# Moving the operand parts fh and fl, and every buffer declared behind them, by 32 bytes in SBUF

## What is computed

```python
x = first_block(x, c, ...)   # adaLN, gated conv + pooling mixer, conv GELU feed-forward
h = x
for i in range(2):
    mix = gated_deltanet(h, ...) if i == 0 else moba_attention(h, ...)
    h = layer_norm_2(ALPHA * h + mix, ...)
    h = layer_norm_2(ALPHA * h + swiglu(h, f_w13[i], f_w2[i]), ...)

def swiglu(x, w13, w2):
    g, u = jnp.split(x @ w13, 2, axis=-1)
    return (jax.nn.silu(g) * u) @ w2
```

## Time and profile before

| | us |
|---|---|
| median of 3 runs | 1084.91 |
| lowest and highest | 1083.35, 1088.65 |
| the profiled execution's own time | 1086.5 |
| its span, first to last instruction | 1084.7 |
| PE busy in the span | 1051.5 (97%), 7748 matmuls |
| DVE busy | 776.6 (72%) |
| ACT busy | 599.3 (55%) |
| DMA moved | 195.47 MB, mean 180 GB/s |
| mean granted TensorE clock | 0.994 of full speed |

### The profile page before, as it was taken

How to read it: one execution, slowest core, us unless ns; L and a number is a source line. 1 busy time by engine, 2 the same in 40 slices (tenths; PEclk the granted TensorE clock), 3 DMA queues, 4 the chain that set the end, 5 groups by cost and what they waited for, 6 DMA issues and landing times.

```text
span 1084.7 us, 18886 instructions
## 1 busy us (share of the span) xinstructions
PE 1051.5 (97%) x7748; PEld 988.8 (91%) x7748; DVE 776.6 (72%) x1327; ACT 599.3 (55%) x1029; POOL 1.3 (0%) x13
## 2 busy tenths in 40 slices
PE   7999998999999999989999999999999999999999
PEld 7999997999999988889987899999899878999997
DVE  7989998788878778676768655555689766555555
ACT  5577555665556567652455654544565656545543
POOL 0000000000000000000000000000000000000000
PEclk9999999999999989999999999999999999999999
DMA  9996574566766523351223555656465436565511
GB/s 373 418 361 201 178 245 156 175 216 238 239 219 198 193 80 115 107 166 60 84 92 110 200 177 192 194 176 195 141 211 173 124 116 247 176 192 190 181 60 39
DMA packets 58021, 195.47 MB, mean 180 GB/s; under 512 B 10320, under 2 KB 10704, under 8 KB 57680
## 3 DMA queue, kind: packets, MB, share of 16 engines
q1 hardware_dynamic: 56784, 194.21, 53.1%
q10 hardware_dynamic: 1152, 0.07, 0.1%
HBM read 192.94 MB, written 1.31 MB: 179 GB/s over the span
## 4 chain that ended last, share of the span: by engine, by line
PE 73%; DVE 18%; ACT 7%; issue 2%; DMA 1%; ACTq 0%; POOL 0%; DVEq 0%; POOLq 0%; SPq 0%
PE ps L551 63%; DVE lo L1748 6%; PE ps L848 3%; ACT hi L1166 2%; PE ps L634 2%; DVE raw L1735 2%; DVE ev L1980 1%; DVE ev L1977 1%; DVE B L2158 1%; DVE sm L1925 1%; PE ps L727 1%; DVE ev L1987 0%; ACT ev L1345 0%; DVE xa L1759 0%; DVE B L1816 0%
## 5 line engine op out<-in xcount | busy, mean ns | idle before, releaser
L1748 DVE TENSOR_TENSOR lo<-raw,hi 128x1024 fp32r<-128x1024 f32 x311 | 376.6, 1221 | 141.9 <-ACT hi L1166 141.2
L551 PE MATMUL ps<-hh,hi 128*128 128x256 f32 x1568 | 445.4, 284 | 9.6 <-DVE hl L1793 3.1
L551 PE MATMUL ps<-hl,hi 128*128 128x256 f32 x1568 | 440.1, 281 | 0.0
L551 PE MATMUL ps<-hh,lo 128*128 128x256 f32 x1568 | 439.9, 281 | 0.0
L1166 ACT ACTIVATE hi<-raw 128x1024 fp32r<-128x1024 f32 x311 | 323.4, 1052 | 50.2 <-PE ps L551 44.6
L551 PEld LDWEIGHTS ps<-hh,hi 128*128 128x128 f32 x1568 | 297.2, 190 | 15.0 <-issue 6.1
L551 PEld LDWEIGHTS ps<-hl,hi 128*128 128x128 f32 x1568 | 297.2, 190 | 1.6
L551 PEld LDWEIGHTS ps<-hh,lo 128*128 128x128 f32 x1568 | 297.0, 189 | 0.0
L551 PE MATMUL ps<-hi,hh 128*128 128x512 f32 x184 | 75.0, 408 | 2.9 <-DVE hl L2022 2.5
L551 PE MATMUL ps<-hi,fh 128*128 128x512 f32 x192 | 76.3, 397 | 0.0
L551 PE MATMUL ps<-lo,fh 128*128 128x512 f32 x192 | 75.9, 395 | 0.0
(11 more groups left out here) (283 smaller groups left out, 1272.2 us busy)
## 6 DMA issues: line engine op xcount, KB each, us to landing
raw<-in_w SPq DMA_DIRECT2D x359, 512.0 KB, 4.3
B<-in_t SPq DMA_DIRECT2D x2, 512.0 KB, 4.8
xa<-in_x SPq DMA_DIRECT2D x1, 1024.0 KB, 11.2
B<-in_r SPq DMA_DIRECT2D x1, 1024.0 KB, 6.1
out<-h SPq DMA_DIRECT2D x4, 256.0 KB, 2.0
cst<-in_c SPq DMA_DIRECT2D x1, 864.0 KB, 9.3
vec<-in_v SPq DMA_DIRECT2D x1, 328.5 KB, 7.7
ev<-between SPq DMA_DIRECT2D x1, 128.0 KB, 2.6
```

What stands on the lines that cost most here:

```text
L551: m = g.matmul(o, l, r, start=first and n == 0, stop=last and n == 2, skip_group_check=True)
L1748: g.tensor_tensor(lo[:, j % SPLIT, :], raw[:, PLACE[j] % RAW, :], hi[:, j % SPLIT, :].bitcast(F), ALU.subtract).then_inc(*up("lo", j))
```

## The change

`gap1` grows from 8 to 16 words, so `fh`, `fl` and everything declared behind them lie 32 bytes further. The four passes of `idle_rows` are taken out. No other instruction, wait or DMA is added, removed or moved.

```diff
         hh = sb("hh", [P, NC, S], FR)
         hl = sb("hl", [P, NC, S], FR)
-        gap1 = sb("gap1", [P, 8])
+        gap1 = sb("gap1", [P, 16])
         fh = sb("fh", [P, 4, S], FR)
         fl = sb("fl", [P, 4, S], FR)
...
             ffn_tokens("w131", "w21", "w13r1", "x5", [[at("att_lo", 4 + 2 * c + half) for half in range(2)] for c in range(2)])
 
-            def idle_rows(shift):
-                wh, wl = (w[:, 0, shift:shift + 512] for w in (hi, lo))
-                for k in range(2):
-                    three(bank[4][:, :], wh, wl, hh[:, k, 0:P], hl[:, k, 0:P], True, True, flip=True)
-
-            for shift in (0, 8, 16, 24):
-                idle_rows(shift)
-
```

## The result

The changed kernel took **1088.59 us** (median of 22 runs, 1085.74 to 1091.47), the kernel before 1086.05 us (22 runs, 1081.33 to 1090.43). The ratio is **1.0023, with a 95% interval of 1.0013 to 1.0033**: some 2.5 us slower, 1.4 to 3.6. That is no tie, but it lies within the 0.5% that I called no change. The forecast was 1085.1 us against 1084.9, +0.2 us. Of the 3.5 us between 1085.1 and 1088.59 the kernel before accounts for 1.1: its median was 1084.91 over three runs and is 1086.05 over 22. The change accounts for the rest.

The account below looks back on a forecast made before the run. PE's matmul streams were taken to bound the kernel from 296 us in the first layer and throughout the later two. Terms -0.3 + 0.5 = +0.2 us on a median of 1084.91 gave 1085.1 us, range 1081 to 1090.

Parts of the forecast that it names:

- the forecast's own case: Down units run as with `hh`: +0.2 us, 1085.1 us for the median; chance 0.60.
- rival (c): Down units of all three layers at 120 and 240 ns, tiles behind at 117.9: +7.5 us, 1092.4; chance 0.13.
- the prediction's own signs: Wrong if down units took 2.72 or 2.88 us for 24, or long-row tiles 2.83; right at 2.80.
- Where a longer matmul costs time: First layer from 296 us, second and third throughout: one for one; before 296 us DVE covers it.
- fh and fl moving, first layer: 264 matmuls of down units behind 296 us go from 117.9 to 116.7 ns: -0.3 us, bounds -1.2 and +0.6.
- all of these now run at 117.9: The first layer's 11 down units behind 296 us, before the change, taken at 117.9 ns a matmul.
- The tiles behind them: Tiles after the down units keep their pattern: 0; if all fell into the slower one, +2.6 us.
- fh and fl stationary: Later layers and half the delta rule's output, 576 matmuls: +0.5 us, bounds -2.6 (228 ns) and +4.3 (240 ns).
- Everything behind fl: Buffers 32 bytes further, for DVE, ACT, DMAs and matmuls with both operands there: 0.
- idle_rows, 0: 24 matmuls at the end that nobody waits for, hidden by DVE's normalisation: 0, or 0.03 us if wrong.
- Rival (a): Addresses don't matter, or a rounding of the layout swallows the 32 bytes: 1084.9 us; chance 0.15.
- Rival (b): Moving reads at 113.3 ns, stationary ones as the last pass of `idle_rows`: -3.8 us, 1081.1; chance 0.12.

Follow-up runs that it names:

- e3: Kernel before without `idle_rows`, `fh` and `fl` 32 bytes further (place 96), buffers behind them 128 bytes further; ratio 1.0022.
- e8: Kernel before without `idle_rows`, `fh` and `fl` moved to place 32, that of `hh`, the rest in place modulo 128; ratio 0.9991.
- e1: Kernel before with only `gap1` grown to 16 words, `idle_rows` kept; ratio 1.0012.
- e12: The kernel of e2 run once more for its profile; no ratio, one run of 1086.76 us.
- e6: Kernel before without `idle_rows`, `gap0` at 40 and `gap1` at 24 words: `hh` and `hl` at place 96, `fh` and `fl` at 192; ratio 1.0086.
- e7: Kernel before without `idle_rows`, `gap0` and `gap1` at 16 words: `hh` and `hl` at place 0, `fh` and `fl` still at 64; ratio 1.0090.
- e4: Kernel before without `idle_rows`, `fh` and `fl` in place, only the buffers behind them 32 bytes further; ratio 0.9999.
- e2: Kernel before with only `idle_rows` taken out; ratio 0.9998.
- e9: Kernel before without `idle_rows`, two views of longer `fh` and `fl` buffers: first layer 192/64 modulo 256, other uses 128/0; ratio 1.0020.
- e11: Kernel before without `idle_rows`, two views of longer `fh` and `fl` buffers: first layer 224/96 modulo 256, other uses 192/64; ratio 0.9998.
- e5: Kernel before without `idle_rows`, `gap0` at 32 words and no `gap1`: `hh` and `hl` at place 64, as `fh` and `fl`; ratio 1.0024.

## Why the prediction was right, and which steps failed

**The time fell into the range, and it was no change of over 0.5%; the forecast's own case did not come.** I had the units behave as `hh` does, +0.2 us. They behaved as in rival (c) for the moving operand, and the change cost 2.5 us. The bounds caught it, the chosen values didn't. By the prediction's own signs it was wrong: down units of 2.86 us, near the 2.88 that it named, and tiles of 2.83 and more in a long row. That the time held is owed to the width of the range and to how few matmuls without slack the change touches, and in that it was luck.

- *Where a longer matmul costs time*: right. From the first down unit to 296 us the layer took 90.49 us after 90.58; behind it the loss came through whole. By the chains, DVE's normalisation begins 78.77 to 79.81 us after the start of the piece in the four executions with `fh` at 64, and 80.72 to 80.77 in the three with it at 96.
- *fh and fl moving, first layer, -0.3 us*: failed, twice. The row of `hh` was chosen because it has the same place modulo 64, so that 96 would act as 32. e3 and e8 refute it: 119.7 ns at 96, 117.0 at 32. The upper bound, the 120 ns of `idle` in the earlier trace rows, was the right row. And "all of these now run at 117.9" held for one execution of the kernel. Over four executions at that place the 11 units have a mean of (113.5 + 117.9) / 2 = 115.7 ns. With it the term is 264 x (119.7 - 115.7) = +1.06 us.
- *The tiles behind them, left at 0*: too low. Behind 296 us 16 tiles of the first layer's ran at 117.8 after the change (18 in e1, 16 in e3), and none in the kernel before (two in e12). 16 x 24 x 1.1 ns = +0.42 us. With the term above that is 1.48 us, against 1.46 measured. The two later layers' tiles did not follow: none of them reached 117.5.
- *fh and fl stationary, +0.5 us*: right, a little high. 576 x 0.59 ns = +0.34 us by the distances, +0.29 by the stretches. The 240 ns of rival (c) did not come; 229.2 in e6 and 226.7 in e7 show that distances about the low bound of 228 exist, for other places.
- *Everything behind fl, 0*, and *idle_rows, 0*: right, as far as e4 and e2 can tell, each to some 1.5 us.
- *Rival (a), addresses don't matter*: falls with e6 and e7. *Rival (b), the new place suits PE*: falls; distances near its 113.3 and 228 ns, 114.2 and 229.2, appear at 192, not at 96.

The mechanism that I gave, two reads of one engine that get in each other's way, is still only argued. What the runs show is that moving the activation buffers in SBUF, with the weights left where they are, changes the distance between starts, at equal clock, columns and type. That rows with equal buffers differed was the warning in the rows of before. I took it for the way a stream begins, and then priced the change by a single execution of it all the same.

## What to carry to other kernels

When PE streams without a gap, read the distance between starts for each kind of operand pair over whole units, and treat the place of each operand buffer as a setting of its own: here steps of 32 or 64 bytes moved it between 113.5 and 120 ns, and a kernel by up to 0.9%. Before a distance is priced, look at several executions of the same program, since a stream can have two patterns and one profile shows one of them, and compare times at equal granted clock. Write an edit that moves one buffer relative to another out modulo at least 256 bytes for every pair, or it may test two things at once, as e9 to e11 did.

## What the runs showed of the hardware that I had not expected

- One kernel, two patterns: at place 64 a unit of 24 matmuls takes 2.73 or 2.83 us, and all 11 units of a stretch can differ together between two executions (e2 and e12, on different chips). This alone moved the stretch behind 296 us by 1.04 us.
- Moving operand, 256 columns, by place: 0 gives 119.7 ns (`hh`), 32 about 117 (both), 64 either 113.5 or 117.9 (`fh`; with `hh` at 64 or 0 nearly always the longer), 96 gives 119.7 (both), 192 gives 114.2 on the mean of the one kernel that had it (`fh`, with `hh` at 96).
- Activation part stationary, 512 columns: 0 gives 228.4 on the mean (`hh`), 32 gives 233.1 to 233.2 (both), 64 gives 232.6 (`fh`; 233.3 and 233.6 in e5 and e7, with `hh` at 64 and 0), 96 gives 233.1 (`fh`), 192 gives 229.2 (`fh`, in e6). Place 0 is among the slowest for one role and the fastest for the other.
- Moving DVE's and ACT's buffers by 32 bytes (e4) changed nothing that the interval of 0.9984 to 1.0013 can show, and matmuls with both operands among them kept their distance.
- The time of an execution follows its mean granted clock, some 0.5 to 0.7 us for each 0.001 of it in e2, e4, e3 and the changed kernel; between the executions of one kernel this moves the time more than the change does.
